# Eight samples' value products in 32-column tiles, three samples side by side, and one conditioning product moved by a unit

## What is computed

```
o, lse = gathered_attn(qa, kfa, vfa, ca_k.shape[1], rel_bias[:, :N_HEADS_A], dil, window // dil, None)  # 3 branches
oa = merge_branches(outs, lses)
ob, _ = gathered_attn(qb, kfb, vfb, cb_k.shape[1], rel_bias[:, N_HEADS_A:], 1, B_WINDOW, sinks)
```

## Time and profile before

| | us |
|---|---|
| median of 3 runs | 2267.2 (2265.6 to 2269.57) |
| the profiled execution | 2266.84 |
| its span, first to last instruction | 2265.1 |
| TensorE busy with products in it | 2161.6 (95%) |
| VectorE, ScalarE, GpSimd busy | 778.9, 580.7, 614.4 |
| chain that ended last: TensorE, VectorE, ScalarE | 87%, 6%, 2% |

### The profile page before, as it was taken

How to read it: one execution, slowest core, us unless ns; L and a number is a source line. 1 busy time by engine, 2 the same in 40 slices (tenths; PEclk the granted TensorE clock), 3 DMA queues, 4 the chain that set the end, 5 groups by cost and what they waited for, 6 DMA issues and landing times.

```text
span 2265.1 us, 33136 instructions
## 1 busy us (share of the span) xinstructions
PE 2161.6 (95%) x13244; PEld 1976.8 (87%) x13244; DVE 778.9 (34%) x1709; ACT 580.7 (26%) x1071; POOL 614.4 (27%) x397
## 2 busy tenths in 40 slices
PE   6799999999999998999979989999999999999997
PEld 2689999999999997998844449899999999999995
DVE  1532122321223229202365652751222211222327
ACT  2311111112111123422265561361111111111114
POOL 1232322223222230124233333132323232323210
PEclk8899999999999999999989999999999999999999
DMA  8372222321321110413242012111111111111002
GB/s 288 131 231 94 84 66 93 112 93 38 112 93 38 47 38 19 148 47 108 101 169 106 1 38 66 38 47 48 56 37 56 37 56 37 56 37 56 28 1 75
DMA packets 168942, 171.36 MB, mean 76 GB/s; under 512 B 14370, under 2 KB 130834, under 8 KB 168324
## 3 DMA queue, kind: packets, MB, share of 16 engines
q1 hardware_dynamic: 168836, 169.84, 23.2%
HBM read 156.91 MB, written 19.20 MB: 78 GB/s over the span
## 4 chain that ended last, share of the span: by engine, by line
PE 87%; DVE 6%; ACT 2%; issue 2%; SPq 2%; DMA 1%; POOL 0%; DVEq 0%; ACTq 0%
PE psum L211 26%; PE psum L213 25%; PE psum L212 25%; PE psum L1086 2%; PE psum L546 2%; PE psum L1145 1%; PE psum L987 1%; DVE NT L694 1%; PE psum L1443 1%; DMA ADA<-in_w_ada 1%; SPq L499 1%; PE psum L644 1%; DVE Y L659 1%; DVE Y L679 1%; PE psum L1136 1%
## 5 line engine op out<-in xcount | busy, mean ns | idle before, releaser
L211 PE MATMUL psum<-Hhi,Whi 128*128 128x344 f32 x2736 | 878.7, 321 | 19.5 <-DVE Hlo L703 10.3
L213 PE MATMUL psum<-Hhi,Wlo 128*128 128x344 f32 x2736 | 875.2, 320 | 0.0
L212 PE MATMUL psum<-Hlo,Whi 128*128 128x344 f32 x2736 | 874.4, 320 | 0.0
L313 POOL TENSOR_TENSOR Wlo<-RAW,Whi 128x1024 fp32r<-128x1024 f32 x158 | 383.2, 2446 | 696.9 <-ACT Whi L309 696.3
L211 PEld LDWEIGHTS psum<-Hhi,Whi 128*128 128x128 f32 x2736 | 515.9, 189 | 29.9 <-issue 23.0
L213 PEld LDWEIGHTS psum<-Hhi,Wlo 128*128 128x128 f32 x2736 | 515.6, 188 | 0.0
L212 PEld LDWEIGHTS psum<-Hlo,Whi 128*128 128x128 f32 x2736 | 514.9, 188 | 0.3
L436 DVE TENSOR_TENSOR GF<-SIL,psum 128x344 f32<-128x344 f32 x132 | 67.6, 512 | 902.7 <-ACT SIL L400 900.1
L443 DVE SCALAR_TENSOR_TENSOR Y<-psum,G,Y 128x344 f32<-128x344 f32 (+1 forms) x528 | 301.2, 573 | 180.5 <-PE psum L213 180.5
L211 PE MATMUL psum<-Ghi,Whi 128*128 128x344 f32 x1056 | 340.2, 322 | 2.4 <-DVE Y L443 2.4
L212 PE MATMUL psum<-Glo,Whi 128*128 128x344 f32 x1056 | 338.0, 320 | 0.0
(11 more groups left out here) (192 smaller groups left out, 1312.0 us busy)
## 6 DMA issues: line engine op xcount, KB each, us to landing
ADA<-in_w_ada SPq DMA_DIRECT2D x38, 1024.0 KB, 9.6
RAW<-in_ffn_wg SPq DMA_DIRECT2D x44, 512.0 KB, 3.8
RAW<-in_ffn_wu SPq DMA_DIRECT2D x44, 512.0 KB, 3.7
RAW<-in_ffn_wd SPq DMA_DIRECT2D x44, 512.0 KB, 3.7
RAW<-in_w_in SPq DMA_DIRECT2D x36, 256.0 KB, 3.2
SK<-in_cache_a_k SPq DMA_DIRECT2D x24, 256.0 KB, 3.5
SK<-in_cache_a_v SPq DMA_DIRECT2D x24, 256.0 KB, 3.7
joint_rows<-joint_heads SPq DMA_DIRECT2D x1, 4608.0 KB, 27.7
```

The source lines that it names most:

```text
L211: pe.matmul(out, whi, xhi, start=first, stop=False)
L212: pe.matmul(out, whi, xlo, start=False, stop=False)
L213: return pe.matmul(out, wlo, xhi, start=False, stop=last)
L313: pool.tensor_tensor(Wlo[slot][:, :, :], RAW[raw][:, :, :], Whi[slot][:, :, :].bitcast(F32), ALU.subtract).then_inc(W[phase].ready, 1)
```

## The change

First, in chunk 0 the first conditioning half goes one unit further on: it stands before unit 4 instead of unit 3. Second, the value products. Samples are now numbered `n = 3 i + j`: `i` is the tile (columns 32i to 32i + 31 of the array, and the slot of `SK`), `j` the group. A group (`VGROUP`: 0, 3, 6; then 1, 4, 7; then 2, 5) is multiplied at one place: for each of the three row sets, the samples of the group side by side, each with 32 weight columns. The B rows of all samples go to the tile of columns 96 to 127, 128 columns of the bank for each `i`, one after each row set. A product of zeros starts that tile's accumulation. A slot is free when both its last A product and its B product are done.

`PZ` is half as large. The picked B rows lie in their own tile `MB`, three times, and `samp_out_pe` has four products with `MA` and twelve with `MB`.

```diff
-                if i == 3 and len(ada) == 2:
+                if i == 4 and len(ada) == 2:
                     ada_pe(pe, *ada[0])
...
-                    samp_values_pe(pe, range(3 * u - 9, min(3 * u - 6, NS)))
+                    samp_values_pe(pe, u - 3)
...
+        VGROUP = [[n for n in range(NS) if n % 3 == j] for j in range(3)]
+        TILE_N = [len([n for n in range(NS) if n // 3 == i]) for i in range(3)]
...
         def samp_values_sp(sp, n):
-
-            if n < 3:
-                sp.wait_ge(red_done, max(m for m in range(NS) if m % 3 == n) + 1)
+            i, j = n // 3, n % 3
+            if j == 0:
+                sp.wait_ge(red_done, max(m for m in range(NS) if m % 3 == i) + 1)
             else:
-                sp.wait_ge(sampv_done, n - 2)
-            samp_load(sp, "v", n, n % 3, sampv_in[n % 3])
+                sp.wait_ge(sampv_done[i], 2 * j)
+            samp_load(sp, "v", n, i, sampv_in[i])
...
+                pe.matmul(bank[7][96:, 0:384], PN[:, 1, 96:], RS[:, 0:384], start=True, stop=False)
+            for n in VGROUP[j]:
+                pe.wait_ge(sampv_in[n // 3], 64 * (j + 1))
+            for s in range(3):
+                for n in VGROUP[j]:
+                    i = n // 3
+                    ins = pe.matmul(bank[7][32 * i:32 * i + 32, :], PZ[:, n, s, :], SK[i][:, s * 512:(s + 1) * 512],
+                                    start=(j == 0 and s == 0), stop=False)
+                    if s == 2:
+                        ins.then_inc(sampv_done[i], 1)
+                if s < len(VGROUP[j]):
+                    n = VGROUP[j][s]
+                    pe.matmul(bank[7][96:, 128 * s:128 * s + 128], PZ[:, n, 3, :], SK[s][:, 1536:], start=False,
+                              stop=False).then_inc(sampv_done[s], 1)
+            if j == 2:
+                for i in range(3):
+                    pe.matmul(bank[7][96:, 128 * i:128 * i + 128], PN[:, 1, 32 * i:32 * i + 32],
+                              RS[:, TVB * P:(TVB + 1) * P], start=False, stop=(i == 2))
+                pe.matmul(bank[7][0:96, :], PN[:, 0, 0:96], RS[:, TVA * P:(TVA + 4) * P], start=False,
+                          stop=True).then_inc(samp_pe, 1)
...
             for t in range(4):
-                src = MAB[:, 2 * t:2 * t + 2, :].rearrange("p h d -> p (h d)")
-                last = pe.matmul(bank[7][:, t * 2 * NS:(t + 1) * 2 * NS], src, who[:, 0:2 * NS], start=True, stop=True)
+                at = 2 * NS * t
+                pe.matmul(bank[7][:, at:at + NS], MA[0:96, 2 * t:2 * t + 2, :].rearrange("p h d -> p (h d)"),
+                          who[0:96, WHO_A], start=True, stop=True)
+                for i in range(3):
+                    last = pe.matmul(bank[7][:, at + NS + 3 * i:at + NS + 3 * i + TILE_N[i]],
+                                     MB[96:, i, 2 * t:2 * t + 2, :].rearrange("p h d -> p (h d)"),
+                                     who[96:, WHO_B:WHO_B + TILE_N[i]], start=True, stop=True)
...
+            dve.memset(PN[:, :, :], 0.0)
             step("pz0", dve.memset(PZ[:, :, :, :], 0.0))
...
+            for i in range(3):
+                last = dve.tensor_tensor(OBG[96:, i, :, :], bank[7][96:, 128 * i:128 * i + 128].rearrange("p (g d) -> p g d", g=2),
+                                         who[96:, 2 * NS + NH:2 * NS + NH + 2].unsqueeze(2).to_broadcast([32, 2, HD]), ALU.mult)
+            step("obg", last)
+            step("obs", dve.tensor_tensor(OBS[96:, :, :], OBG[96:, :, 0, :], OBG[96:, :, 1, :], ALU.add))
+            for i in range(3):
+                for g in range(2):
+                    last = dve.tensor_tensor(MB[96:, i, :, :].rearrange("p (t s) d -> p s t d", s=2)[:, g],
+                                             OBS[96:, i, :].unsqueeze(1).to_broadcast([32, 4, HD]),
+                                             who[96:, 2 * NS + 4 * g:2 * NS + 4 * g + 4].unsqueeze(2).to_broadcast([32, 4, HD]),
+                                             ALU.mult)
...
-            for n in range(3, NS):
+            for n in VGROUP[1] + VGROUP[2]:
                 samp_values_sp(sp, n)
```

More of the change, by code:

```diff
@@ L111, in constants @@
     who = np.block([[own, none, head], [none, own, head]]).astype(np.float32)
+    rows = np.zeros((P, NS + 3), np.float32)
+    for n in range(NS):
+        rows[32 * (n // 3) + 8 * (n % 3):32 * (n // 3) + 8 * (n % 3) + NH, n] = 1.0
+    for j in range(3):
+        rows[96 + 8 * j:96 + 8 * j + NH, NS + j] = 1.0
+    who = np.concatenate([who, rows], axis=1)
     return {"const_hot": hot, "const_joint": joint, "const_who": who}
@@ L1290, in build @@
         SNEWT = arena.at("SNEWT", [NS, 2, NH], F32, o); o += 4 * 2 * NH
-        MAB = arena.at("MAB", [P, NH, HD], F32, o); o += 4 * NH * HD
+        MB = arena.at("MB", [P, 3, NH, HD], F32, o); o += 12 * NH * HD
         assert o <= BIG + 4 * T * (TVA + 4)
         o = PROJ_END
-        PZ = arena.at("PZ", [P, NS, 4, ROWS], F32, o); o += 4 * NS * 4 * ROWS
-        PN = arena.at("PN", [NS, 2, ROWS], F32, o); o += 8 * ROWS
+        PZ = arena.at("PZ", [P, NS, 4, 32], F32, o); o += 4 * NS * 4 * 32
+        PN = arena.at("PN", [NS, 2, P], F32, o); o += 8 * P
+        MA = arena.at("MA", [P, NH, HD], F32, o); o += 4 * NH * HD
         assert o <= PROJ_END + 10592
         o = BIG + 4 * T * TVB
[L1299 to L1302, removed]
+        OBG = arena.at("OBG", [P, 3, 2, HD], F32, o)
+        OBS = arena.at("OBS", [P, 3, HD], F32, o + 1536)
+        DN = arena.at("DN", [ROWS, 2, NS], F32, o + 2304)
+        WHO_A = slice(2 * NS + NH + 2, 3 * NS + NH + 2)
+        WHO_B = 3 * NS + NH + 2
+        who = arena.at("who", [P, WHO_B + 3], F32, o + 2368)
         MAX_, NEGM, DEN, RDEN = (slice(2 * i, 2 * i + 2) for i in range(4))
@@ L1312, in build @@
         samp_tables = sem("samp_tables")
-        prd_done, red_done, sampv_done = sem("prd_done"), sem("red_done"), sem("sampv_done")
+        prd_done, red_done = sem("prd_done"), sem("red_done")
+        sampv_done = [sem(f"sampv_done{i}") for i in range(3)]
+        VGROUP = [[n for n in range(NS) if n % 3 == j] for j in range(3)]
+        TILE_N = [len([n for n in range(NS) if n // 3 == i]) for i in range(3)]
         def cache_rows(name, n, step):
@@ L1433, in samp_rows_turn_pe, with samp_values_pe @@
             last.then_inc(samp_pe, 1)
-        def samp_values_pe(pe, samples):
-            if samples[0] == 0:
+        def samp_values_pe(pe, j):
+            if j == 0:
                 pe.wait_ge(samp_dve, samp_at["pz"])
[L1438 to L1447, removed]
+                pe.matmul(bank[7][96:, 0:384], PN[:, 1, 96:], RS[:, 0:384], start=True, stop=False)
[18 more added lines that the diff above has]
+                          stop=True).then_inc(samp_pe, 1)
         def samp_out_pe(pe):
@@ L1538, in samp_pick_dve @@
             dve.wait_ge(samp_pe, 5)
[L1539 to L1548, removed]
+            own = who[0:96, 2 * NS:2 * NS + NH].unsqueeze(2).to_broadcast([96, NH, HD])
+            step("ma", dve.tensor_tensor(MA[0:96, :, :], bank[7][0:96, :].rearrange("p (h d) -> p h d", d=HD), own, ALU.mult))
+            for i in range(3):
+                last = dve.tensor_tensor(OBG[96:, i, :, :], bank[7][96:, 128 * i:128 * i + 128].rearrange("p (g d) -> p g d", g=2),
+                                         who[96:, 2 * NS + NH:2 * NS + NH + 2].unsqueeze(2).to_broadcast([32, 2, HD]), ALU.mult)
+            step("obg", last)
+            step("obs", dve.tensor_tensor(OBS[96:, :, :], OBG[96:, :, 0, :], OBG[96:, :, 1, :], ALU.add))
+            for i in range(3):
+                for g in range(2):
[3 more added lines that the diff above has]
+                                             ALU.mult)
             step("mb", last)
@@ L1663, in _ @@
                 kv_sp(sp, b)
-            for n in range(3):
+            for n in VGROUP[0]:
                 samp_values_sp(sp, n)
```

9 lines of the change are left out of this document (6 added, 3 removed).

## The result

The changed kernel took 2277.49 us (median of 6 runs, 2275.68 to 2279.58); the kernel before, in the 6 runs beside it, 2268.3. The ratio is 1.003, 95% interval 1.0018 to 1.0042: **slower by 6.8 us (4 to 9.5)**. The prediction said 2267.3 and no change that can be told; the time lies above its range, 2261.5 to 2272.5. The profiled execution took 2279.58 us, its span is 2277.8, and TensorE is busy for 2165.1 us of it (2161.6 before).

What follows compares the result with a forecast made beforehand. It took TensorE to carry the chain, its clock below full at both places; -0.6 - 11.4 + 3.5 + 1.4 + 2.3 + 1.6 + 3.6 = +0.4 us gave 2267.3 us, range 2261.5 to 2272.5.

Steps and rivals of the forecast that it cites:

- conditioning half: Chunk 0: the half at full clock saves 2.9 us, a restart in unit 5 costs 2.3; -0.6 (-1.4 to 0).
- value products at full clock: Three groups behind units 3, 4 and 5 take 10.4 us together instead of 21.8, side by side; -11.4 us.
- wait for the loads behind unit 4: TensorE waits there for the twelfth load of group 1; +3.5 us (2.5 to 4.2).
- restart at half clock behind it: After the wait behind unit 4 the clock restarts at half; +2.3 us (0 to 2.9).
- picking: Before the way out, six `MB` instead of two, 0.38 us each, stand behind the larger `OBS`; +1.6 us.
- the way out: `samp_out_pe`: 32 passes at 0.13 us and eight changes of form take 4.7 us; +3.6 (+1.3 to +7.4).
- The chunk 0 chain: About 1 us of gap stays before the first half; one of about 9 appears before unit 5, released by `GF`.
- rival (4): Chunk 0: unit 5 isn't held, so 8.66 - 1.1 + 2.9 us are gained; 2257 us, chance 0.04.
- the last kind lands 4.1 us after issue: Loads behind unit 4: with issuing, the twelfth lands 9.2 us after the group, 3.2 too late.
- rival (2): Behind the waits and way out the clock keeps falling (+2.3) and out products stand alone (+3.8); 2273.5 us, chance 0.14.
- (1): Value products and way out: costs at their lower ends, clock up over the 3.5 us wait; 2261 us, chance 0.17.
- (3): Value products: four tiles do not run side by side, so the 11.4 us go away; 2278 us, chance 0.03.

Runs made afterwards that it cites:

- e10_after_again: The changed kernel once more, unedited, for a second profile; one execution, 2278.74 us.
- e2_values_only: The changed kernel with the first conditioning half of chunk 0 back before unit 3; 2277.79 us, ratio 1.0026 to the kernel before.
- e3_no_reload: As e2_values_only, but the values of samples 1, 2, 4, 5, 7 are not loaded; 2269.92 us, ratio 0.9996 to the kernel before.
- e5_half_and_pieces: Kernel before, first conditioning half before unit 4, pieces 0 and 1 of chunk 1 fetched ahead of the second half's tiles; 2263.68 us, ratio 0.9962.
- e9_half_bytes: The changed kernel, loads for groups 1 and 2 fetching half the columns in as many transfers; one execution, 2273.09 us.
- e4_out_in_8: As e2_values_only, but picked B rows gathered in one tile, so the way out has 16 passes instead of 32; 2269.82 us, ratio 0.9996.
- e6_groups_apart: As e4_out_in_8, groups in the middle of units 3 and 5 and behind unit 6, way out at unit 7's end; 2267.27 us, ratio 0.9983.
- e7_all: As e6_groups_apart, plus the two edits of e5_half_and_pieces; 2256.74 us, ratio 0.993 to the kernel before.
- e12_all_but_apart: As e4_out_in_8, plus the two edits of e5_half_and_pieces; 2261.03 us, ratio 0.995 to the kernel before.
- e8_pieces_only: The kernel before with only the order of fetches of e5_half_and_pieces, first half still before unit 3; 2270.38 us, ratio 0.9992.
- e1_half_only: The kernel before with one edit, the first conditioning half of chunk 0 before unit 4; 2273.58 us, ratio 1.0004.
- e11_before_again: The kernel before once more, unedited, for a second profile; one execution, 2267.92 us.

## Why the prediction failed, point by point

| term, us | predicted | measured |
|---|---|---|
| conditioning half | -0.6 | -0.4 |
| value products at full clock | -11.4 | -11.1 |
| wait for the loads behind unit 4 | +3.5 | +5.6, +5.2, +5.1 |
| restart at half clock behind it | +2.3 | +2.9, +1.6, +1.7 |
| wait for the loads behind unit 5 | +1.4 | +1.6, +1.6, +2.5 |
| half clock behind unit 5 | 0 | 0, 0, +1.7 |
| picking | +1.6 | +1.5 |
| the way out | +3.6 | +4.1, +5.2, +4.5 |
| half clock behind the way out | 0 | +2.3, +2.7, +1.9 |
| sum, with means | +0.4 | +6.8 |

Three values are those of after, `e10_after_again` and `e2_values_only`. The groups at full clock: 3.5, 2.7 (in `e3_no_reload`) and 4.5, 10.7 us for 21.8. The restart: the group behind the wait took 5.27 instead of 2.7, and 0.33 more for the eight products behind it (1.46 and 1.13); in the other two profiles the clock was back sooner, and the group took 4.35 and 4.40. In the third it fell again behind unit 5 (6.2 us instead of 4.5). Picking: the wait before the way out was 2.26 in the last two, 0.77 in the kernel before; in after it was 0.77 again, but there unit 6 ran at half clock, TensorE came as much later, and VectorE's `MB` ended on the same schedule. The sum meets the ratio's 6.8; it is made of single profiles, so take it to half a microsecond or so.

**The chunk 0 chain, right.** Unit 3 ran in the gap before the half (2.1 us of it left, 1.1 foretold), and the new gap before unit 5, its length and its releaser came as told; rival (4) fell. `e5_half_and_pieces` showed the cause itself.

**The step that failed first: "the last kind lands 4.1 us after issue".** The prediction counted the loads by the SP queue's issue times and one landing time, both taken from rows in which four transfers went out at a time, and took a middle value for twelve without pauses. Twelve in a row are bound by their bytes: the DMA engines were 0.93 busy, landings grew to 4.7 us in the median and 6.2 at most, and TensorE waited 5.6 us instead of 3.5, above the upper bound of 4.2. `e9_half_bytes` settled it. The trace of before had the rate, in its busiest stretch of these loads:

```profile
1180.50:1184.50 4.00, 4.00 (x27) 2.37 (x25) 1.81 (x9) 0.60 (x1) 0.00 (x0) 1.00 0.87 283
```

2.56 MB at 283 GB/s take 9.0 us, and with the 2.5 us of the shortest landing of an A transfer there 11.5: against the 6.0 of a unit, a wait of 5.5.

**The second: the way out, and the clock behind it.** 32 passes at 0.13 were right for as long as the clock stood: three of four quarters. But the prediction kept the clock up through them, although it had seen in rival (2) what could come: "the clock keeps falling". It fell in all three profiles inside the way out, in its second, third or last quarter, and took 2.3 us from the work behind. `e3_no_reload` shows that it needs no wait for loads; what stood ahead of the way out there was the 2.26 us for VectorE. With 32 passes the loss, in the way out and behind it, was 3.2 to 4.7 us in all five profiles. With 16 it was 0 in `e4_out_in_8` (no wait before, but the clock had just fallen in unit 6), and 3.3, 1.8 and 1.6 us in `e6_groups_apart`, `e7_all` and `e12_all_but_apart` (waits of 1.9, 1.9 and 0.8 us); the first two have the same attention code. So fewer passes seem to make it smaller, but the two ranges touch, and how much is the wait's, the short products' or the single execution's these runs don't tell apart.

In size this step is the larger one: of the 6.4 us between the two sums, 3.3 lie in the way out and behind it, 2.3 in the two waits, the rest in small differences.

**Which rival.** (2) named the mechanism and gave 2273.5, at 0.14. It had one restart more as a case by itself; the way out had no drain of its own at full clock (0.13 us a pass), so that part of it did not come. (1) and (3) fell: no cost came at its low end, and the tiles ran side by side. The 18 passes of a group take 2.71 us at full clock where they took 7.8, a factor of 2.9. The Trainium skill (TensorE: Matmul & The Clock Gate, "Measured speedup vs the span model") has 2.38 for three column tiles; by that the groups would have taken 1.6 us more, and the trace does not agree.

**The chances.** The wait was bounded from landings of lighter traffic and came out above its bound; the way out came within its bounds (+1.3 to +7.4), and the half clock behind it had no term outside rival (2), so no bound covered it. The sum explains 6.8 of the 9.2 us between the medians. The rest isn't placed; the interval of the difference, 4 to 9.5, holds it, and the base of 2267.2 was the median of three, where later runs had 2272 for the same kernel. (The forecast also mixes two bases: +0.4 on the median of 2267.2 is 2267.6, not 2267.3, which decides nothing.)

## What to carry over

Before you group transfers that used to be spread, cost them by bytes over the rate that the trace shows for the same kind of transfer in its busiest stretch (283 GB/s here, where other transfers of this kernel reached 418), not by issue count and a landing time from a quiet stretch; then place the groups at least that far apart. A saving on TensorE is only worth what is left when the next wait and the lower clock behind it are paid; a pass of a short product took about the same here, 0.11 to 0.13 us, for 3, 8 or 16 columns, so gather such products over partitions first (`e4_out_in_8`, 6.8 us). And an edit worth nothing by itself may be half of a pair: the half moved (0) and the fetches reordered (-1.8, not told from 0) gave 8.6 us together.

## What the runs showed that I had not expected

- VectorE reads rows 96 to 127 and writes rows 0 to 31, 32 to 63 or 64 to 95 in the same instruction (`OBG` in `e4_out_in_8`), at 0.91 us for three, where three that stay in their rows took 0.72.
- The same 24 `Hlo` subtractions, whose own code no edit touched, take 10.6 to 11.0 or 14.7 to 14.9 us. In the short case GpSimd's two splits beside them took 8.54 us, in the long case single ones took 2.4; which engine gives way differs from run to run. Why was not tried. It also moved the end less than it seems: from the last values of the attention to the end it took 920.1 and 922.4 us in the two profiles of before, 923.9 in `e8_pieces_only` (short) and 925.5 in `e1_half_only` (long).
- The first conditioning half starts when `ADA` lands, and that was anywhere from 90.4 to 94.3 us of the span in fourteen profiles, a spread of 3.9 us that no edit set. (The 30.3 to 34.7 us in the expectation of `e11_before_again` count from a product near 60 us, not from the start of the chunk.)
